# Two-matmul weight tiles: the remainder product ahead of the rounded one at odd tiles

## The reference

```python
# first block
proj = h @ w_in
y_ret = (silu(g_ret) * ret) @ w_ret_out
glu_a, glu_b = split(y_ssm @ w_s5_glu, 2)
y = merged @ w_out
x = x + gt_f * rmsnorm((silu(a) * b) @ w_ffn_out, g[3])      # a, b = split(h @ w_ffn_in, 2)
# second block
proj = h @ w_in
mixed = g0 * (o_a @ w_br_attn) + g1 * (o_g @ w_br_gla) + g2 * (y_c @ w_br_conv)
x = x + mixed @ w_out
x = x + (silu(h2 @ w_ffn_gate) * (h2 @ w_ffn_up)) @ w_ffn_down
```

## Time and profile before

| | us |
|---|---|
| median of 3 runs | 3386.57 (3383.78 to 3386.83) |
| profiled execution, its own time | 3381.64 |
| profiled execution, span from first to last instruction | 3379.9 |
| PE (matmul) busy | 3307.3 |
| PE weight load busy | 2937.2 |
| VectorE busy | 2324.5 |
| ScalarE busy | 1452.4 |

### The profile page before, as it was taken

One profiled execution on the slowest core, in us unless ns is written; L12 is line 12 of the kernel. 1 busy time (PEld: TensorE's weight loads), 2 busy tenths in 40 slices (PEclk: granted clock), 3 DMA queues, 4 the chain that ended last, 5 costly groups with the idle time before them and its releaser, 6 DMA issues.

```text
span 3379.9 us, 51972 instructions
## 1 busy us (share of the span) xinstructions
PE 3307.3 (98%) x20368; PEld 2937.2 (87%) x20368; DVE 2324.5 (69%) x2503; ACT 1452.4 (43%) x1464; POOL 435.2 (13%) x309
## 2 busy tenths in 40 slices
PE   6999999999899999999899999999999999999998
PEld 3599999999788888888788888888888888888887
DVE  6789979877766666666666667566767766666554
ACT  2256664444443444433454443444344444344332
POOL 1047668500100000000000000000003000000000
PEclk9999999999999999999999999999999999999999
DMA  9885456678545555577534444555555555555554
GB/s 378 349 328 180 180 202 237 251 292 311 198 175 188 192 191 186 195 268 254 198 137 169 167 162 178 193 183 186 192 186 196 188 188 186 189 192 186 185 191 149
DMA packets 119746, 706.34 MB, mean 209 GB/s; under 512 B 13776, under 2 KB 28752, under 8 KB 41312
## 3 DMA queue, kind: packets, MB, share of 16 engines
q1 hardware_dynamic: 109280, 695.96, 56.2%
q10 hardware_dynamic: 10368, 9.02, 0.8%
HBM read 702.83 MB, written 2.10 MB: 209 GB/s over the span
## 4 chain that ended last, share of the span: by engine, by line
PE 90%; DVE 5%; ACT 1%; DMA 1%; SPq 1%; issue 1%; DVEq 0%; ACTq 0%
PE acc L638 45%; PE acc L639 24%; PE acc L635 6%; PE acc L636 6%; PE acc L637 6%; DVE ring_raw L1499 1%; DVE ring_lo L1477 1%; DMA ring_raw<-w_ada 1%; SPq L542 1%; PE p_y L705 1%; PE p_norm L687 1%; PE p_z L715 1%; ACT ring_hi L1017 0%; DMA ring_raw<-w_out 0%; DVE rstd L1524 0%
## 5 line engine op out<-in xcount | busy, mean ns | idle before, releaser
L638 PE MATMUL acc<-h_split,ring_hi 128*128 128x512 f32 x4736 | 1655.9, 392 | 9.5 <-DVE h_split L1539 4.5
L1477 DVE TENSOR_TENSOR ring_lo<-ring_raw,ring_hi 128x2048 fp32r<-128x2048 f32 (+2 forms) x560 | 1265.1, 2260 | 550.2 <-ACT ring_hi L1017 549.1
L639 PE MATMUL acc<-h_split,ring_lo 128*128 128x256 f32 x4736 | 1337.6, 282 | 0.0
L1017 ACT ACTIVATE ring_hi<-ring_raw 128x2048 fp32r<-128x2048 f32 (+2 forms) x560 | 1040.0, 1862 | 458.6 <-DMA ring_raw<-w_down 150.4
L638 PEld LDWEIGHTS acc<-h_split,ring_hi 128*128 128x128 f32 x4736 | 891.9, 188 | 197.6 <-issue 10.0
L639 PEld LDWEIGHTS acc<-h_split,ring_lo 128*128 128x128 f32 x4736 | 897.9, 190 | 0.4
L638 PE MATMUL acc<-ffn_split,ring_hi 128*128 128x512 f32 x1408 | 488.2, 390 | 0.0
L2146 POOL TENSOR_TENSOR sq_sum<-sq_sum,tile 128x256 f32<-128x256 f32 x60 | 79.6, 1326 | 2561.6 <-ACT tile L1043 2561.6
L639 PE MATMUL acc<-ffn_split,ring_lo 128*128 128x256 f32 x1408 | 397.1, 282 | 0.0
L635 PE MATMUL acc<-h_split,ring_hi 128*128 128x256 f32 x1152 | 329.2, 286 | 0.3 <-ACT val_a L1030 0.2
L637 PE MATMUL acc<-h_split,ring_lo 128*128 128x256 f32 x1152 | 321.6, 279 | 0.0
(11 more groups left out here) (381 smaller groups left out, 3936.5 us busy)
## 6 DMA issues: line engine op xcount, KB each, us to landing
ring_raw<-w_ff SPq DMA_DIRECT2D x88, 1024.0 KB, 4.8
ring_raw<-w_down SPq DMA_DIRECT2D x64, 1024.0 KB, 4.8
ring_raw<-w_ffb SPq DMA_DIRECT2D x56, 1024.0 KB, 4.8
ring_raw<-w_mix SPq DMA_DIRECT2D x48, 1024.0 KB, 4.8
ring_raw<-w_ada SPq DMA_DIRECT2D x32, 1024.0 KB, 11.9
ring_raw<-w_heads SPq DMA_DIRECT2D x32, 1024.0 KB, 4.8
ring_raw<-w_ret SPq DMA_DIRECT2D x32, 1024.0 KB, 5.2
ring_raw<-w_glu SPq DMA_DIRECT2D x32, 1024.0 KB, 4.9
```

Of the source, the lines that this page charges most:

```text
L638: mm(dst[:], hi[s][:, t, :], moving[:, k, :], start=start, stop=False, skip_group_check=True)
L639: return mm(dst[:, T:], lo[s][:, t, :], moving[:, k, 0:T], start=False, stop=stop, skip_group_check=True)
L1017: run(hi[s][:, 0:n, :], raw[s][:, 0:n, :], COPY).then_inc(hi_done, 1)
L1477: tt(lo[s][:, 0:n, :], raw[s][:, 0:n, :], hi[s][:, 0:n, :], SUB).then_inc(lo_done, 1)
```

## The change

At even t the order stays: line 638's product, then line 639's. At odd t the remainder weights' product of 256 columns is issued first, and the product of 512 columns second. The stop flag goes to whichever is last, and that instruction is the one returned, on which signals are put. The start flag stays on the 512-column product; it is only set at t = 0, which is even.

```diff
-                mm(dst[:], hi[s][:, t, :], moving[:, k, :], start=start, stop=False, skip_group_check=True)
-                return mm(dst[:, T:], lo[s][:, t, :], moving[:, k, 0:T], start=False, stop=stop, skip_group_check=True)
+                def whole_hi(stop):
+                    return mm(dst[:], hi[s][:, t, :], moving[:, k, :], start=start, stop=stop, skip_group_check=True)
+
+                def half_lo(stop):
+                    return mm(dst[:, T:], lo[s][:, t, :], moving[:, k, 0:T], start=False, stop=stop, skip_group_check=True)
+
+                if t % 2:
+                    half_lo(False)
+                    return whole_hi(stop)
+                whole_hi(False)
+                return half_lo(stop)
```

## The result

The changed kernel takes 3404.52 us (median of 6 runs, 3398.01 to 3413.21), the kernel before 3386.70 (also six runs): a ratio of 1.0056, 95% interval 1.0041 to 1.0072. The change makes the kernel 18 us slower. The forecast was no difference, 3386.5. The time lies just inside the stated range of 3345 to 3405, and on the side to which only 0.22 had been given. The profiled execution took 3400.78 us, with a span of 3399.0.

The account below looks back on a forecast made before the run. The prediction took PE's matmul stream as the bound, 6784 pairs at 346.6 ns, about 2351 us. Waits, column order and starts summed to 0, leaving the median of 3386.57, so 3386.5 us was forecast, range 3345 to 3405.

Parts of the forecast that it names:

- What bounds the kernel: Whole kernel: PE's matmul stream sets the end almost without idling; what remains is the distance between starts, 346.6 ns a pair.
- Waits: Two-matmul stages: odd tiles ask for nothing earlier, and all waits stand ahead of both matmuls of a tile: 0.
- column order: Upper half of the bank: adding again to the same columns after 256 column times is no hazard: 0.
- the end of a block: Block's last matmul: the slot_free signal comes after 508 ns instead of 510, 0 to within 2 ns.
- The joints of products: Where products meet, two 512-column matmuls now adjoin: at most 8 ns at each of 392 products, 3 us.
- Starts: Two-matmul stages: equal-size neighbours pay what alternating ones pay, since each matmul keeps one load under it: 0 us.
- a toll that belongs to each load: PE at full clock: each matmul with its load costs about 13.3 ns beyond its columns, 26.6 ns a pair.
- the slower rival: Two-matmul stages: closely following loads under two small products delay the large one; 4.4 ns a pair, +30 us, 3416; chance 0.22.
- its half price: Only tiles after two small products in a row pay the delay: +15 us, 3401.
- The faster rival: Two-matmul stages: matmuls following their own size start sooner; -11 to -34 us, 3352 to 3375, at lowest 3341; chance 0.35.
- What would show it: Timeline of ff2: small-to-small 117 to 120 ns, large-to-large 227 to 230, two pairs 693; a sequence-dependent rhythm would refute it.

Follow-up runs that it names:

- the three-matmul experiment: Against the kernel before, the 512-column product is split into two of 256 columns, each with its own weight load, in every stage: 3411.73 us, ratio 1.0077.

## Why the prediction was wrong, point by point

*What bounds the kernel: right.* PE's stream sets the end in both kernels, no wait has come in, and the difference is in the distance of starts.

*Waits, column order, the end of a block: right, all 0.* PE idles 9.4 us against 9.5. Nothing points to a cost of adding S to the columns of the S before it: from the first S to the next B it takes 0.23 us in the long rhythm and 0.24 in the short one. The joints of products, for which up to 3 us were allowed, show no loss either: in the new order B meets B there as it does between any odd tile and the next.

*Starts: wrong, and this is the step that failed.* It said that in the new order "every matmul still has exactly one load under it, so B B and S S pay what B S and S B pay", a sum of 0. That holds for the short rhythm, where B B S S takes 693.3 ns as 2 x 346.7 did. But the sequence has a second steady period, 706.7 ns, and in both traces the 2112 pairs of ff2 and down2 were in it, 14.1 us. The premise under it, a toll that belongs to each load, fell with the three-matmul experiment: 350 ns with three loads in the feed-forward stages, where it asks for 360. The stated range held the number only because it had been drawn wide enough to take in half of the slower rival.

*The size of the slower rival.* It had the right sign, and one of its marks was right: over 347.6 ns a pair, with the loss behind two S in a row and under B, where the two distances sum to 0.47 us, 235 ns each against the 231 or more that it named. It was mis-sized in both factors: 4.4 ns a pair on all pairs or on half of them, where it is 6.7 ns on about a third of them in both traces. That its half price, 3401 us, comes near the measured time is luck. Its mechanism, loads that spill over because they follow each other too closely, is not supported: the same loads at the same distance run in the short rhythm when one matmul is put into the break. It also named out2 as the model, and out2 itself became faster: 348.3 ns a pair by the starts in the trace, where it had 351.0.

*The faster rival.* No two-matmul stage went under 346.7 ns, not even in runs of four of one size, which took 350.0.

*What it had seen and not used.* The last sentence of "What would show it" named the right doubt, a rhythm that depends on the sequence of sizes. The earlier trace rows held the evidence: one instruction form at 113.3, 116.7 and 120 ns in one execution, 3.3 ns apart, with nothing waited for. Such steps could have said that a stream settles into one of a few periods, and that a new sequence may have periods of its own. 0.22 was too little for that.

*What stays open.* Why the stream has these periods at all, and why a break sets one or the other: by the moment of the restart or by the number of matmuls in the break. The runs show that in ff2 the choice hangs on what PE does in the break, and that it then holds for hundreds of us over more than a hundred products. Around that break PE is not idle in these traces, and the same program gave the same rhythm there in both traces. The places where executions of one program differ, out1 and the first feed-forward part, come behind waits of PE for VectorE; that the waits make the difference is likely and not shown. Of the 18 us of the first group of runs 14 are explained. Three of its six runs took 3398 to 3401 us and three 3408 to 3413; when the changed kernel ran again, all four took 3396 to 3403. The three long ones weren't traced. With both feed-forward parts long a run would take 3412 to 3415 us, which fits the longest, 3413.21, and not the two at 3408 and 3409.

## What to carry to other kernels

When PE is never idle and the kernel is still slower, count matmuls in equal windows stage by stage, and measure a steady period over some fifty repeats in the timeline: here a difference of 2% in matmuls, under an unchanged clock and without a wait, was a rhythm. Reordering matmuls that PE executes anyway is not free of risk even if all columns and loads stay: alternate large and small ones, as in the kernel before, had 346.7 ns a pair in every stage but out2 in all traces, and pairs of equal size had a second, longer period, of which a whole stage may be made. Look at several executions before judging such a change, since a single trace shows one draw.

## What the runs showed of the hardware that was not expected

At a granted clock of 1.00, streams of fp32r products with one load each had periods that came in steps. For 768 columns they were 346.7, 350.0 or 353.3 ns, and for 256 columns 113.3, 116.7, about 118 or 120. Most of these periods lie 3.3 or 6.7 ns apart. The columns alone, at the pace of the earlier trace rows doubled, would be 320 and 106.7. One extra fp32 matmul in a break of 0.90 us, which made it 1.23 whether it had 32, 64 or 128 columns, moved the following 720 us of work from one step to the other, and two of 128, which made it 1.46, did not. One stage of 256-column products ran at 113.3 or about 118 ns in executions of one and the same program.
